# Hybrid decoder layer: down projection of the sample rows with both parts in one stationary operand, and three orders of instructions

## What is computed

```
z = rmsnorm(x) @ W_in            # combined projection, 2312 columns used
A = windowed attention with sinks (8 heads);  B = mLSTM, chunkwise (4 heads)
x = x + [rmsnorm(A) || rmsnorm(o * B)] @ W_out
x = x + relu(rmsnorm(x) @ W_up)^2 @ W_down      # W_up 1024x4096, W_down 4096x1024
y = rmsnorm(x)
```

## Time and profile before

| | us |
|---|---|
| median of 3 runs | 2432.26 |
| lowest and highest | 2429.77, 2432.62 |
| profiled execution, its time | 2429.19 |
| profiled execution, its span | 2427.4 |
| PE busy, PEld busy | 2378.6, 2017.0 |
| DVE busy, ACT busy, POOL busy | 1359.0, 961.3, 75.9 |
| mean granted TensorE clock | 0.997 |

### The profile page before, as it was taken

The page is one execution under the profiler, slowest core; times in us unless marked ns, Lnnn a source line. Parts: engine busy times, 40 slices in busy tenths (PEclk is TensorE's granted clock), DMA queues, the critical chain, the costliest instruction groups (busy, mean ns, idle before and its releaser), DMA issues.

```text
span 2427.4 us, 33523 instructions
## 1 busy us (share of the span) xinstructions
PE 2378.6 (98%) x13125; PEld 2017.0 (83%) x13125; DVE 1359.0 (56%) x3109; ACT 961.3 (40%) x2049; POOL 75.9 (3%) x131
## 2 busy tenths in 40 slices
PE   7999999999999999999999999999999999999998
PEld 6988788888897888888998888888889879888886
DVE  4478544546368654446356854444656765444444
ACT  4345433334345533334334543333433544233331
POOL 1000000000000000000000400000010000000000
PEclk9999999999999999999999999999999999999999
DMA  6312323233411232334421233323343112222221
GB/s 182 86 45 85 97 96 96 96 113 120 145 54 53 87 98 93 97 95 131 147 67 36 71 102 96 96 95 113 118 130 110 47 49 93 79 79 79 81 85 57
DMA packets 178266, 224.35 MB, mean 92 GB/s; under 512 B 18123, under 2 KB 129044, under 8 KB 178092
## 3 DMA queue, kind: packets, MB, share of 16 engines
q1 hardware_dynamic: 165596, 189.82, 25.5%
q10 hardware_dynamic: 6560, 22.55, 2.6%
q0 software_dynamic: 5952, 9.83, 1.5%
HBM read 210.78 MB, written 12.60 MB: 92 GB/s over the span
## 4 chain that ended last, share of the span: by engine, by line
PE 93%; DVE 4%; issue 1%; ACT 1%; DMA 0%; ACTq 0%; DVEq 0%
PE ps L1881 28%; PE ps L1883 28%; PE ps L1882 28%; PE ps L1960 2%; PE ps L1940 1%; PE ps L1949 1%; DVE w_lo L1095 1%; PE ps L2006 1%; DVE w_lo L1099 1%; PE ps L2009 1%; PE ps L1921 1%; PE ps L1909 0%; PE ps L1985 0%; DVE wide L1479 0%; PE ps L2016 0%
## 5 line engine op out<-in xcount | busy, mean ns | idle before, releaser
L1881 PE MATMUL ps<-a_hi,w_hi 128*128 128x512 f32 (+2 forms) x1704 | 592.2, 348 | 11.6 <-DVE w_lo L1095 5.9
L1883 PE MATMUL ps<-a_hi,w_lo 128*128 128x512 f32 (+2 forms) x1704 | 593.6, 348 | 0.0
L1882 PE MATMUL ps<-a_lo,w_hi 128*128 128x512 f32 (+2 forms) x1704 | 591.7, 347 | 0.0
L1883 PE MATMUL ps<-w_hi,u_lo 128*128 128x512 f32 (+1 forms) x1088 | 429.0, 394 | 0.0
L1881 PE MATMUL ps<-w_hi,u_hi 128*128 128x512 f32 (+1 forms) x1088 | 428.9, 394 | 0.0
L1882 PE MATMUL ps<-w_lo,u_hi 128*128 128x512 f32 (+1 forms) x1088 | 426.2, 392 | 0.0
L665 ACT ACTIVATE w_hi<-w_raw,gains 128x256 fp32r<-128x256 f32 (+1 forms) x576 | 252.9, 521 | 418.5 <-PE ps L1883 418.5
L1881 PEld LDWEIGHTS ps<-a_hi,w_hi 128*128 128x128 f32 x1704 | 322.5, 189 | 55.0 <-DVE w_lo L1099 5.3
L1882 PEld LDWEIGHTS ps<-a_lo,w_hi 128*128 128x128 f32 x1704 | 320.8, 188 | 41.0
L1883 PEld LDWEIGHTS ps<-a_hi,w_lo 128*128 128x128 f32 x1704 | 321.1, 188 | 39.4
L1103 DVE TENSOR_TENSOR x<-x,ps 128x512 f32<-128x512 f32 x272 | 185.4, 685 | 278.1 <-PE ps L1883 278.0
(11 more groups left out here) (323 smaller groups left out, 2159.7 us busy)
## 6 DMA issues: line engine op xcount, KB each, us to landing
w_raw<-in_w_up_dram SPq DMA_DIRECT2D x128, 512.0 KB, 3.7
w_raw<-in_w_down_dram SPq DMA_DIRECT2D x128, 512.0 KB, 3.5
w_raw<-in_w_out_dram SPq DMA_DIRECT2D x32, 512.0 KB, 3.5
w_raw<-in_w_in_dram SPq DMA_DIRECT2D x24, 580.0 KB, 5.0
w_raw<-in_w_in_dram SPq DMA_DIRECT2D x24, 512.0 KB, 3.8
w_raw<-in_w_in_dram SPq DMA_DIRECT2D x32, 256.0 KB, 3.1
x<-in_x_prompt_dram ACTq DMA_DIRECT2D x12, 512.0 KB, 6.7
wide<-in_x_prompt_dram ACTq DMA_DIRECT2D x12, 512.0 KB, 4.6
```

The lines of the kernel that those rows point to most:

```text
L1881: eng.matmul(out, lh, rh, start=(k == ks[0]), stop=False)
L1882: eng.matmul(out, lh, rl, start=False, stop=False)
L1883: ins = eng.matmul(out, ll, rh, start=False, stop=(k == last))
```

## The change

It does five things (in the diff, three identical lines `u_hi, u_lo = u_views(last)` at the heads of the engines' `quarter` are left out).

1. `u_views` lays the hidden values out anew for quarter 3: each row of `u_hi` gets 64 more columns behind the sample's 64, and they hold the sample's low part; `u_lo` keeps only the prompt's 512. So DVE's `low` is two instructions where a piece reaches past column 512. The sample tile's gemm becomes `gemm_both`: 128 stationary columns, high and low side by side, times `w_hi` and then `w_lo`, which is 4 x 2 matmuls. The result stands in 128 PSUM rows, and DVE adds it to `x1` in two instructions with a semaphore wait between them. (The product of low and low, left out before, is now in it.)
2. DVE's splitting of the running maximum (`split_max`) moves from the end of block 1 to block 2, behind `take_turned`.
3. In the first M step DVE makes both halves of the next unit's `w_lo` before the first hidden piece.
4. At the O stage's end the order of norms, low parts, bank readings and the two halves of `split(U_M)` is changed on DVE, and in quarters 0 to 2 on ACT too, where half 0 goes ahead of `high_tile(1)`.
5. `op_step(o)` goes ahead of `low_heads(q, 1)`.

```diff
@@ -228,8 +228,7 @@
         phase = ExitStack()
-        u_hi = [sb(f"u_hi{b}", [P, 4, TMAX], F32R, phase) for b in range(2)]
-        u_lo = [sb(f"u_lo{b}", [P, 4, TMAX], F32R, phase) for b in range(2)]
+        u_all = sb("u_all", [P, 4 * 4 * TMAX], F32R, phase)
         relu = sb("relu", [P, 2, TMAX], where=phase)
@@ -437,6 +436,13 @@
             return a * b // 2
+
+        def u_views(last):
+
+            hi, lo = (TMAX + NS, TQ) if last else (TMAX, TMAX)
+            n = 8 * hi
+            return ([u_all[:, b * 4 * hi:(b + 1) * 4 * hi].rearrange("p (k t) -> p k t", k=4) for b in range(2)],
+                    [u_all[:, n + b * 4 * lo:n + (b + 1) * 4 * lo].rearrange("p (k t) -> p k t", k=4) for b in range(2)])
@@ -943,11 +950,14 @@
                     square_tile(q, NT, 2)
-                high_tile(q, NT, 1)
-                split_act(eng, q, last, U_M, 0)
-                split_act(eng, q, last, U_M, 1)
-                if last:
+                    high_tile(q, NT, 1)
+                    split_act(eng, q, last, U_M, 0)
+                    split_act(eng, q, last, U_M, 1)
                     high_tile(q, NT, 2)
+                else:
+                    split_act(eng, q, last, U_M, 0)
+                    high_tile(q, NT, 1)
+                    split_act(eng, q, last, U_M, 1)
                 square_tile(q, NT, NT - 2)
@@ -1260,6 +1270,9 @@
                 stabilise(q, BLK, P, mp[:, 0:BLK].unsqueeze(2).broadcast_to([HM, BLK, P]), buffers, Mrel, lambda r: rows[r:r + HM, :, :], r_rows, vec)
+
+            def split_max(q):
+
                 eng.wait_ge(r_rows.sem, r_rows.at(q, 1))
@@ -1685,6 +1699,8 @@
                     take_turned(q, j)
+                    if j == 2:
+                        split_max(q)
                     if j:
@@ -1748,8 +1764,8 @@
                     low_heads(q, 0)
+                op_step(o)
                 low_heads(q, 1)
-                op_step(o)
                 split_vec(eng, q, U_O + 3, 0)
@@ -1772,18 +1788,25 @@
                     op_at(3, BLK)
-                op_at(2, 2)
-                norm_tile(q, NT, 1)
-                low_tile(q, NT, 0)
-                op_at(2, 3)
-                if last:
+                    norm_tile(q, NT, 1)
+                    low_tile(q, NT, 0)
+                    op_at(2, 2)
                     norm_tile(q, NT, 2)
-                low_tile(q, NT, 1)
-                split_vec(eng, q, U_M, 0)
-                op_at(3, 2)
-                split_vec(eng, q, U_M, 1)
-                if last:
+                    low_tile(q, NT, 1)
+                    op_at(2, 3)
+                    split_vec(eng, q, U_M, 0)
+                    op_at(3, 2)
+                    split_vec(eng, q, U_M, 1)
                     low_tile(q, NT, 2)
+                else:
+                    op_at(2, 2)
+                    norm_tile(q, NT, 1)
+                    low_tile(q, NT, 0)
+                    op_at(2, 3)
+                    split_vec(eng, q, U_M, 0)
+                    low_tile(q, NT, 1)
+                    split_vec(eng, q, U_M, 1)
+                    op_at(3, 2)
                 op_at(3, 3)
@@ -1795,6 +1818,8 @@
                         split_vec(eng, nq, nu, 0, i)
+                    if u == U_M:
+                        split_vec(eng, nq, nu, 1, i)
                     if u == UNITS - 4 and not last:
@@ -1808,7 +1833,11 @@
                             eng.wait_ge(u_high.sem, u_high.at(q, o + 1))
-                            tt(u_lo[b][:, half * 2 + t, off:off + w], usq[:, l % 2, 0:w], u_hi[b][:, half * 2 + t, off:off + w].bitcast(F32), ALU.subtract).then_inc(u_split.sem, 1)
+                            n = min(w, TQ - off)
+                            ins = tt(u_lo[b][:, half * 2 + t, off:off + n], usq[:, l % 2, 0:n], u_hi[b][:, half * 2 + t, off:off + n].bitcast(F32), ALU.subtract)
+                            if n < w:
+                                ins = tt(u_hi[b][:, half * 2 + t, TMAX:TMAX + NS], usq[:, l % 2, n:w], u_hi[b][:, half * 2 + t, TQ:TMAX].bitcast(F32), ALU.subtract)
+                            ins.then_inc(u_split.sem, 1)
@@ -1820,7 +1849,7 @@
                             low(l, o, t, off, w)
-                            if n == NN - 1 and not end:
+                            if n == NN - 1 and not end and u != U_M:
                                 split_vec(eng, nq, nu, 1, i)
@@ -1828,7 +1857,12 @@
                             xs = x1[0:R, j, half * 512:half * 512 + 512]
-                            tt(xs, xs, ps[4 + o % 4][0:R, :], ALU.add).then_inc(dn_read.sem, 1)
+                            ins = tt(xs, xs, ps[4 + o % 4][0:R, :], ALU.add)
+                            if j == BLK:
+                                ins.then_inc(vec.sem, 1)
+                                eng.wait_ge(vec.sem, vec.next(q))
+                                ins = tt(xs, xs, ps[4 + o % 4][NS:2 * NS, :], ALU.add)
+                            ins.then_inc(dn_read.sem, 1)
                             if n == 1 and not end:
@@ -1881,6 +1915,13 @@
                     ins = eng.matmul(out, ll, rh, start=False, stop=(k == last))
+                return ins
+
+            def gemm_both(out, lhs, rhs, ks):
+
+                for k in ks:
+                    for part, right in enumerate(rhs(k)):
+                        ins = eng.matmul(out, lhs(k), right, start=(k == ks[0] and part == 0), stop=(k == ks[-1] and part == 1))
                 return ins
@@ -2332,7 +2374,10 @@
                             eng.wait_ge(dn_read.sem, dn_read.at(q, max(o - 3, 0)))
-                            ins = gemm(ps[4 + o % 4][0:R, :], lambda k: (u_hi[b][:, k, j * P:j * P + R], u_lo[b][:, k, j * P:j * P + R]), lambda k: w_at(u, k, 0, 512), range(4))
+                            if j < BLK:
+                                ins = gemm(ps[4 + o % 4][:, :], lambda k: (u_hi[b][:, k, j * P:j * P + P], u_lo[b][:, k, j * P:j * P + P]), lambda k: w_at(u, k, 0, 512), range(4))
+                            else:
+                                ins = gemm_both(ps[4 + o % 4][:, :], lambda k: u_hi[b][:, k, TQ:TMAX + NS], lambda k: w_at(u, k, 0, 512), range(4))
                             ins.then_inc(dn_out.sem, 1)
```

More of the change, by code:

```diff
@@ L791, in quarter @@
                 T, tiles, splits = tokens_of(last)
+                u_hi, u_lo = u_views(last)
                 NT, NN = len(tiles), len(splits)
```

## The result

The changed kernel takes 2406.62 us (median of 4 runs, 2406.43 to 2409.16), the kernel before 2431.07 us (4 runs, 2429.77 to 2432.62). The ratio is 0.9901, with a 95% interval of 0.9887 to 0.9915: 24.4 us less. In the profiled executions the span went from 2427.4 to 2404.8 us, 22.6 less. The forecast was 24.8 us less and a median of 2407.5. The median lies in the forecast's range.

A forecast was written before the change was run, and what follows sets the result against it. PE, busy 98% of the span, bounds the kernel, with some waits. Terms -13.1 - 4.2 - 3.4 - 0 - 3.7 - 0.4 = -24.8 us take 2429.2 to 2404.4; plus 3.1, median 2407.5 (own range 2405 to 2410; 8 in 10: 2402.5 to 2414).

The forecast's parts named there:

- Part 1: Sample's down tiles, quarter 3: 15 tiles each 0.92 us shorter, last one 0.7 us longer; 13.1 us less.
- the rival's 6.9 us: Follow-up with 64 stationary columns: if loads count, 128 loads x 0.054 us make it 6.9 us faster; no chance given.
- Part 2: Maximum's split moved off PE's wait for the attention values: 1.05 us earlier in each of four quarters, -4.2 us.
- Part 3: First M step, quarters 0 to 2: PE's wait for the half behind the hidden piece goes, 1.13 us each, -3.4 us.
- Part 4a: O stage's end, quarters 0 to 2: 0.69 us wait for the split's second half goes, lost again at the turn; 0.
- Part 4b: O stage's end, quarter 3: waits of 2.41 us for tile 1's norm and 0.94 for the half go; -3.7 us.
- Part 5: Sample's reading ahead of the heads' low part: PE stops again one gemm later; -1.3 or +0.4 us, taken as -0.4.
- I count both alike: Sample's reading: clock falling or not behind the new wait weighted equally, +0.4 or -1.3 us, giving -0.4.
- The loads: Rival: weight loads set the down tiles' pace, so they gain only 0.9 us; 2419.7 us, 4 in 100.
- the slower case: Rival: DVE's paired addings come late at sample tiles, PE stops, its clock falls; 61.6 us cost, 2469 us, 2 in 100.
- The third: Rival: the turn after the O stage, quarters 0 to 2, isn't late and no clock falls; 2404.4 us, 12 in 100.
- Waits move instead of going: Rival: 11.3 us of gains from removed waits are half lost at the next DVE wait; 2413 us, 12 in 100.

The follow-up runs named there:

- parts 3 and 4b undone: Changed kernel with the old first-M-step order of low-part halves and quarter 3's old O-stage order of norms and readings: 2416.26 us, ratio 0.9940 to the kernel before.
- the repeated runs of the changed kernel: The changed kernel, unaltered, run again beside the last experiments on the same chip as the measure for small differences: 2406.93 us.
- part-2-undone kernel: Changed kernel with the running maximum's split back at the end of block 1: 2408.55 us, a single execution.
- part 1 alone: Kernel before plus only the sample's side-by-side high and low parts and second adding, all orders as before: 2417.42 us, ratio 0.9947.
- part 5 undone: Changed kernel with the sample's reading of unit 1 again behind the low part of the second block's heads: 2404.99 us, ratio 0.9895 to the kernel before.
- both moves: Changed kernel, tile 2 turned six matmuls later in quarters 0 to 2, sample's unit 2 reading before heads' low part and unit 3's split in quarter 3: 2401.18 us.

## Why the prediction was right, step by step

- **Part 1 (-13.1).** Right in every piece: 1.85 us for a sample tile, cover ahead of the pair, the last pair on the path (+0.7), loads hidden. Alone on the chip it is 13.1. The load grows with its columns, by less than in proportion (188 against 135 ns), but it is hardly what PE waits for: 0.9 of the rival's 6.9 us shows.
- **Part 2 (-4.2).** The four waits are gone, 3.56 - 2.34 = 1.2 us of lead in quarter 1 (700.61 against the earlier trace rows's 704.17; 242.13 against 244.47 at the same matmul before it), where the forecast left 0.12 of the wait standing. POOL's later copies cost nothing. Whether the part also brings on the fall at 1782 is open.
- **Part 3 (-3.4).** 4.60 - 3.51 = 1.1 us in quarter 1, with no new wait: right.
- **Part 4a (0).** The step that a reader would most easily have counted as a gain of 2 us. The forecast followed the moved reading to ACT's square and to the turn, 3.12 us on, and had 0. The trace has +0.8 and -0.8, the kernel without it the same time.
- **Part 4b (-3.7).** The wait of 2.41 us at the turn (2.6 from start to start) is gone, and from the turn to the first MLP matmul the lead grows from 8.3 to 9.5 us: 3.8, right. That such a wait can also cost a fall of the clock, as with parts 3 and 4b undone, wasn't counted; it makes the part worth more.
- **Part 5 (-0.4).** The mechanism was right: the stop moves one gemm on and is 2.6 us long. The term was mis-sized. The -1.3 took the new order without a fall against the old one with it. Like with like it is +0.4 with a fall in both, as the prediction's own rows say, and nothing with a fall in neither; and its kernel is not faster than the one without it (2406.93 against 2404.99). The step "I count both alike" failed: a fall behind the new stop came in eight of nine traces.
- **What was left out.** The clock's fall at 1782, 1.7 us, at a place where nothing was changed. By terms: 13.1 + 4.2 + 3.4 + 3.7 - 1.7 - 0.4 = 22.3, and the spans have 22.6. The medians have 24.4: the profiled execution of before was at the low end of its runs (2429.19 against a median of 2431.07), that of the change at its median. The forecast's 2404.4 for a profiled execution was 2.2 us too low (2406.58), and the 3.1 us put on top for the median didn't come. So the closeness of 24.8 to 24.4 is partly luck of 2 us (beside the repeated runs of the changed kernel the difference is 2430.60 - 2406.93 = 23.7); the parts that could be read from the trace are right to within some 0.2 us each, but for the clock.
- **Rivals.** The loads and the slower case fell (addings hidden, no wait of PE for x in quarter 3's MLP). The third fell on both counts: PE waits 0.6 us at the turn, and the clock falls twice. "Waits move instead of going" holds for 4a and 5, as forecast, and for no other part. Seen as forecast: all rows named at the end of the prediction.

## What to carry to other kernels

When the small group of rows needs products of its high and its low part with the same moving operand, put both parts side by side in one stationary operand: here a matmul of 512 moving columns took 0.23 us with 64 stationary columns or 128, and the second adding cost nothing where DVE had 1.16 us of idle time ahead of it. Before an earlier release of one wait is counted, follow every instruction that it is moved past: in 4a the moved reading fed a square, a norm and a turn, and the gain ended there. A stop that is only moved can get longer, and what lies in front of a reading that frees a bank (here a split of weights that nobody needed yet) is where to look: moving the reading ahead of it brought 4 us, more than the whole of part 5 could.

## What the runs showed of the hardware

- The clock fell to half speed at 1782 us in the changed kernel though PE had no idle time in front: for 6.4 us before, it had only small matmuls (64 stationary columns and 129 or 32 moving ones, in groups of 4 and 32 in the timeline). In the kernel before, at the same 6.4 us of work 6.6 us later, it didn't fall, nor in the part-2-undone kernel. What decides it is open.

```profile
1776.85 1.98 PE L2129 MATMUL ps<-x,wide 64*64 64x129 f32 x32
1778.76 0.31 PE L2148 MATMUL ps<-PT,om 128*64 128x32 f32 x4
1778.99 0.30 PE L2151 MATMUL ps<-PT,vv 64*64 64x32 f32 x4
...
1782.54 0.64 PE L1915 MATMUL ps<-a_hi,w_hi 128*128 128x512 f32 x1
```

- A fall is not a property of one order alone. Four of 14 traces (before, part 1 alone, part 2 undone, part 5 undone) have none near 1782; the other ten do. Of twelve stops of 2.2 to 2.6 us at the sample's reading nine were followed by one. Each is worth 1.6 to 1.7 us (3.4 in one trace, that of both moves), as much as a whole part of this change, and the program's first 30 us differ by up to 1.3 us among these traces, so that a difference below 2 us between two versions should be read from waits in the trace and not from medians.
